# Gated memory two heads at a time, output products rounded, norms behind the products

## The chip, the cores and the metric

One NeuronCore of a Trainium2 chip runs the whole program. The time is that of the device, in microseconds (us), and for each kernel the median of its runs is given. Before the change: 3743.09 us, the median of 3 runs (3741.81 to 3745.54).

## What is computed

A sequence of 512 tokens of width 1024 passes through two blocks of two layers each. All of it is float32.

```
first block, per layer:   h += 0.5 g1 * swiglu(norm(h)...)      # FFN, width 2816
                          h += g2 * mixer(norm(h)...)           # fox + DSA heads (hyb), then MLA
                          h += 0.5 g3 * swiglu(norm(h)...)
                          ... at the end h = norm(h) * final_g
second block, per layer:  u = norm(h) * norm1_g ;  y = u @ w_in
                          h += concat(gated memory, diff attention, gated recurrence) @ w_out
                          h += relu(norm(h) * norm2_g @ w_up)**2 @ w_down
gated memory, per head:   D[t,s] = b_t - b_s + i_s   (s <= t)
                          S = (q k' / 8) * exp(D - m_t)
                          out = (S v) / max(|sum_s S|, exp(-m_t)),  then a norm and a gate
```

A norm divides each token's row by the root of the mean of its squares. It is a factor per token, so it can be applied to `u` before a product or to `y` behind it.

## The kernel before

**Layout.** The residual `h` is held as 8 chunks of 128 features by 512 tokens, and so is `u`, the input of a layer; `big` holds 32 such chunks. A layer is a list of weight slabs (`ORDER`): SP loads them into a ring of four slots, each load waiting until the slab four places back is done (`lin_done`). PE makes a group of products per slab into one of two PSUM pairs (`LP[0]`, `LP[1]`), DVE takes the group out (`lin_taken0`, `lin_taken1`) and PE may use the pair again.

**Rounded products.** In most layers (`CUT`) each f32 operand is split in a rounded high part and the remainder, and a product is made as three passes: high by high, high by low, low by high (`products`, L474). ACT rounds the weights (`high`, L1062, a copy into `w_hi`, two homes in turn, which waits until the slab two places back *in the list of rounded slabs* is done), and POOL subtracts (`rest`, L1419) in place over the ring (`w_lo`, `w_cut`). The output layers `hybo`, `mlao`, `wo0`, `wo1` (four slabs each, 64 products of 128x512) are not split: PE multiplies in f32 straight from the ring.

**A norm.** When a chunk of `h` is final, ACT squares it (`hrms`, L1107), POOL adds the squares (`squares`, L1468), PE sums over partitions (`total_sum`, L542), ACT takes the root, DVE the reciprocal (`root_total`), PE spreads it over the partitions (`spread`, L555), DVE scales the 8 chunks (`scale_in`, L1625), ACT rounds each, and only then PE starts the next layer's first slab with high passes and, at its end, the low ones (L502). The parameter `cut_at` says ahead of which chunk's square the first two slabs of the next layer are rounded; ACT and POOL keep the same order. In front of the second block two such norms follow each other: the final one of the first block and norm1 of layer 0.

**Attentions.** `duo_attention` (fox and DSA heads) takes two heads in a step: scores in both row halves of the array, and value products in both column halves. `attention` (MLA, diff) takes one. Each step goes PE, DVE, ACT, DVE, PE, ACT, PE.

**Gated memory** (L999 to L1013 for PE, L1376 for ACT, L2251 for DVE). 16 steps, one for each head and block of 128 keys. PE spreads the head's gate row once a head; per step DVE adds the causal mask to one block, ACT makes `E = exp(gate + bias)` (two instructions), PE the scores (64 rows), DVE `S = scores * E / 8`, PE the numerators (64 output rows) and the denominators (4 output rows). Between the steps stand the norms of the other two mixers: six sums (n = 5), a root and a reciprocal, and six spreads and scalings, one a step (n = 8 to 13). Then `out_products` makes the output layer: chunks 2 to 7 of slabs 0 and 1, between them the sum and the spread of the numerators' norm, then chunks 0 and 1, then slabs 2 and 3.

**Order.** Every engine has its program written out by hand; the semaphores named above are the only order between them. Each queue is in order.

Of the kernel before, what the change touches and what calls it, by code (L numbers as in the profile page):

```python
# [27 lines left out]
P = 128  # L28
# [135 lines left out]
class Fresh:  # L164


    def __init__(self, high, first):
        self.high, self.first = high, first
# [17 lines left out]
def build(nc, x, small, consts, consts2, pos, adab, w, out):  # L186
    with ExitStack() as ctx:
# [109 lines left out]

        def root4(b=0, n=1):
            return st[:, 58 + b:58 + b + n]
# [40 lines left out]
        def ffn_order(up, down, ada, more=0):  # L340
# [4 lines left out]
        ORDER += [("hyb", 10, DC * 256, 0, 1), ("hybv", 4, DC * 256, 0, 1), ("hybo", 4, DC * 256, 0, 0)]  # L345
        ORDER += ffn_order("gu01", "dn01", FC // 2) + ffn_order("gu10", "dn10", FC // 2)
        ORDER += [("mlad", 3, DC * 256, 0, 1), ("mlaq", 6, 3 * 256, 0, 0), ("mlak", 4, 2 * 256, 0, 0),
                  ("mlav", 4, 2 * 256, 0, 0), ("mlao", 4, DC * 256, 0, 0)]
        ORDER += ffn_order("gu11", "dn11", 0)
        for l in range(DEPTH):  # L350
            ORDER += [(f"in{l}", 11, DC * 256, 0, 1), (f"inv{l}", 4, DC * 256, 0, 1), (f"wo{l}", 4, DC * 256, 0, 0)]
            for part in "ab":
                ORDER += [(f"up{l}{part}", 8, DC * 256, 0, 1), (f"down{l}{part}", DC, 16 * P, 0, 1)]
# [3 lines left out]
        CUT_SLABS, slabs = [], 0  # L357
        for name, n, width, _, two in ORDER:
            CUT_SLABS += [(slabs + k, width) for k in range(n if two else 0)]
            slabs += n  # L360

# [5 lines left out]
        def peeled(pl, name, n, n_ada):  # L367

            if name in SLAB_ORDER:
                return n  # L370
            return 4 if pl.slab == 0 else n_ada if 0 < n_ada < n else None
# [83 lines left out]
        def _(pe):  # L455
# [11 lines left out]
            def linear(name, kind, src, after=None, fresh=None, amid=None):  # L467
# [13 lines left out]
                def body(k, it):  # L481
# [4 lines left out]
                    if cut:  # L486
                        pe.wait_ge(s("w_cut"), at(pl.cut + k + 1, it, RING))
                        high, rest = w_hi[:, (pl.cut + k) % 2, 0:width], w_lo[:, slot, 0:width]
# [13 lines left out]
                    elif kind == "fm" and k == 0 and fresh is not None:  # L502
# [39 lines left out]
            def total_sum():  # L542
# [3 lines left out]
                pl.got("squares_summed")  # L546
                for b in range(NB):
                    mm(XB[1][:, b:b + 1], sqa[:, blk(b)], cc("ones", 0, 1), start=b == 0, stop=False)
                pl.got("h_squared", DC)
                for b in range(NB):  # L550
                    last = mm(XB[1][:, b:b + 1], sq[:, (DC - 1) % 2, blk(b)], cc("ones", 0, 1), start=False, stop=b == NB - 1)
# [3 lines left out]
            def spread():  # L555

                pe.wait_ge(s("rstd_ready"), pl.norm)
                for b in range(NB):
                    last = mm(XB[0][:, blk(b)], root4(b).to_broadcast([P, P]), cc("ident"))
                last.then_inc(s("rstd_spread"), 1)  # L560

            def norm(high, summed=False):
# [5 lines left out]
                pl.ur += DC  # L568

                def src(c):  # L570
                    return high[:, c, :], u_lo[:, c, :]
                return src, fresh
# [200 lines left out]
            linear("hybo", "fm", lambda c: u[:, c, :])  # L773
# [60 lines left out]
            linear("mlao", "fm", lambda c: u[:, c, :])  # L834
# [4 lines left out]
            total_sum()  # L839
            spread()  # L840
            for l in range(DEPTH):
                src, fresh = norm(u_hi2)
# [127 lines left out]
                u0 = l * 4 * NB  # L970

                def weighted(n):

                    hh, b = divmod(n, NB)
                    pe.wait_ge(s("ms_ready"), u0 + n + 1)
                    mm(XB[hh // 2][half(hh), b * P:T], xv[:, b, 64 * hh:64 * hh + 64], S[:, n % 2, 0:T - b * P],
                       start=b == 0, stop=b == NB - 1)
                    mm(XB[2][0:4, b * P:T], full_sums(hh, 4), S[:, n % 2, 0:T - b * P],
                       start=n == 0, stop=n == 4 * NB - 1).then_inc(s("m_out"), 1)

                def mix_norms(n):

                    if n == 5:
                        pl.got("mix_squared", 3)
                        for c in range(DIFF_H):
                            mm(XB[3][0:8, :], full_sums(c, 8), Z[:, c, :], start=c == 0, stop=False)
                        for cp in range(2):
                            last = mm(XB[3][0:8, :], half_sums(2 + cp, 8), tabs[:, 2 + cp, :], start=False, stop=cp == 1)
                        last.then_inc(s("mix_summed"), 1)
                    if 8 <= n < 14:  # L990
                        i = n - 8
                        if i == 0:
                            pl.got("mix_recip")
                        else:
                            pe.wait_ge(s("mix_scaled"), 6 * l + i)
                        weights = cc("ident")[0:8, i:i + 1].to_broadcast([8, P]) if i < DIFF_H else halves_of(i - 2)
                        mm(XB[3][:, :], weights, mix_rows).then_inc(s("mix_spread"), 1)

                for n in range(4 * NB + 1):  # L999
                    hh, b = divmod(n, NB)  # L1000
                    if n < 4 * NB:
                        if b == 0:
                            if l * 4 + hh:
                                pe.wait_ge(s("g_taken"), l * 4 + hh)
                            mm(LP[1][:, 0, :], cc("ident")[0:4, hh:hh + 1].to_broadcast([4, P]),
# [1472 lines left out]
```

## Time and profile before

| | |
|---|---|
| median of 3 runs | 3743.09 us |
| profiled execution | 3749.99 us |
| its span | 3748.2 us |
| mean granted clock of TensorE | 0.963 |
| PE busy | 3597.0 us (96%) |
| DVE, ACT, POOL busy | 37%, 26%, 40% |

The profile is of one execution, and its own time stands 6.9 us above the median. A granted clock of 1.00 is 2.4 GHz, 0.50 is 1.2 GHz. An f32 product leaves two matmul records, a rounded pass one. The length of a matmul record includes its way through the array, so spacings are read from the starts.

### The profile page before, as it was taken

Reading aid. Unit: us, or ns where it says so; the run is one execution under the profiler, and the core shown is the slowest. Engines: PE = TensorE matmul, PEld = TensorE weight load, DVE = VectorE, ACT = ScalarE, POOL = GpSimd, SP = SyncE. Lnnn points to the kernel's source line nnn. Section 1 sums busy time; section 2 is a strip of 40 time slices with the busy share of each in tenths; the row PEclk is TensorE's granted clock in tenths of the full one; section 3 lists DMA queues with packets and bytes.
Section 4 is the critical chain, followed back from the end, with each engine's and each line's share of the span. In section 5 each row is a group of like instructions: output and inputs, shape, how many; then the busy total and the mean of one; then the engine's idle time right before and its main releaser. Section 6 shows DMA issues by size and latency. Waiting matters only on the chain.

```text
span 3748.2 us, 41071 instructions
## 1 busy us (share of the span) xinstructions
PE 3597.0 (96%) x16200; PEld 2740.0 (73%) x16200; DVE 1385.3 (37%) x2572; ACT 965.4 (26%) x1205; POOL 1490.6 (40%) x521
## 2 busy tenths in 40 slices
PE   8999999799999999999999989989999999799999
PEld 7878777558887888755688866843888869437887
DVE  4454277624243422233210145752201267632010
ACT  2222222522223212303222233331212233312221
POOL 3445451025454545400354554401546445014453
PEclk9999998899999999999999989988999999799999
DMA  6434221025343433220223222101222212002222
GB/s 247 184 140 177 98 79 57 1 79 191 119 190 114 189 123 136 81 99 12 79 80 105 88 76 79 68 1 45 90 91 100 90 68 79 12 34 79 101 90 79
DMA packets 53863, 360.58 MB, mean 96 GB/s; under 512 B 5968, under 2 KB 6352, under 8 KB 16592
## 3 DMA queue, kind: packets, MB, share of 16 engines
q1 hardware_dynamic: 53712, 358.53, 26.4%
q8 instruction: 100, 1.64, 0.2%
q14 instruction: 51, 0.42, 0.0%
HBM read 356.41 MB, written 2.10 MB: 96 GB/s over the span
## 4 chain that ended last, share of the span: by engine, by line
PE 90%; DVE 6%; ACT 1%; issue 1%; DMA 1%; POOL 1%; SPq 0%; DVEq 0%; ACTq 0%; POOLq 0%
PE LP L459 80%; PE XB L459 9%; DVE S L1814 1%; PE LP L747 1%; DMA big<-w_ada 1%; PE XB L631 0%; ACT E L1060 0%; DVE tmp L1936 0%; DVE st L1934 0%; POOL wk L1481 0%; ACT sq L1060 0%; DVE wk L1834 0%; DVE gain L1651 0%; DVE stat L1826 0%; POOL w_lo L1423 0%
## 5 line engine op out<-in xcount | busy, mean ns | idle before, releaser
L1423 POOL TENSOR_TENSOR w_lo<-ring,w_hi 128x2048 fp32r<-128x2048 f32 (+1 forms) x263 | 1122.9, 4270 | 682.8 <-ACT w_hi L1060 682.0
L459 PE MATMUL LP<-u_hi,w_hi 128*128 128x512 f32 x2480 | 992.9, 400 | 21.2 <-ACT u_hi L1060 17.0
L459 PE MATMUL LP<-u_hi,w_lo 128*128 128x512 f32 x2480 | 980.5, 395 | 0.0
L459 PE MATMUL LP<-u_lo,w_hi 128*128 128x512 f32 x2480 | 937.6, 390 | 0.0
L459 PE MATMUL LP<-big_r,w_hi 128*128 128x512 f32 x2432 | 749.6, 389 | 1.2 <-POOL w_lo L1423 1.2
L1060 ACT ACTIVATE w_hi<-ring 128x2048 fp32r<-128x2048 f32 (+1 forms) x263 | 468.7, 1782 | 813.9 <-PE LP L459 726.1
L459 PEld LDWEIGHTS LP<-u_hi,w_hi 128*128 128x128 f32 x2480 | 475.5, 192 | 137.3 <-issue 39.1
L459 PEld LDWEIGHTS LP<-u_hi,w_lo 128*128 128x128 f32 x2480 | 474.9, 192 | 102.2
L459 PEld LDWEIGHTS LP<-u_lo,w_hi 128*128 128x128 f32 x2480 | 467.0, 188 | 95.2 <-issue 0.5
L459 PEld LDWEIGHTS LP<-big_r,w_hi 128*128 128x128 f32 x2432 | 455.9, 188 | 95.6 <-issue 1.3
L459 PE MATMUL LP<-big_r,w_lo 128*128 128x512 f32 x1216 | 473.2, 389 | 0.0
L1464 POOL TENSOR_TENSOR big_r<-tmp,big_r 128x512 f32 (+2 forms) x120 | 192.5, 1604 | 687.6 <-DVE big_r L1667 687.6
L1481 POOL TENSOR_TENSOR wk<-wk,sq 128x512 f32<-128x512 f32 x66 | 84.7, 1284 | 697.2 <-ACT sq L1060 694.2
L1060 ACT ACTIVATE tmp<-LP 128x512 f32<-128x512 f32 (+1 forms) x121 | 86.1, 711 | 971.1 <-PE LP L459 971.1
L1672 DVE TENSOR_TENSOR tmp<-tmp,LP 128x512 f32<-128x512 f32 x88 | 60.6, 688 | 635.1 <-ACT tmp L1060 620.7
L459 PEld LDWEIGHTS LP<-big_r,w_lo 128*128 128x128 f32 x1216 | 228.3, 188 | 47.7
L459 PE MATMUL LP<-u,ring 128*128 128x512 f32 x512 | 224.7, 600 | 4.2 <-DVE u L2284 2.6
L1580 DVE SCALAR_TENSOR_TENSOR XB<-ada_in,csil,XB 128x256 f32<-128x256 f32 x390 | 191.1, 490 | 13.7
L459 PEld LDWEIGHTS LP<-u,ring 128*128 128x128 f32 x512 | 97.7, 192 | 128.8 <-issue 122.6
L1742 DVE SCALAR_TENSOR_TENSOR h<-LP,gate,h 128x512 f32 (+1 forms) x64 | 48.1, 751 | 357.0 <-PE LP L459 356.5
L1060 ACT ACTIVATE E<-S,stat 128x128 f32<-128x128 f32 (+3 forms) x160 | 89.2, 558 | 241.4 <-DVE stat L1817 161.8
L2296 DVE TENSOR_TENSOR tmp<-tmp,LP 128x1024 f32<-128x1024 f32 x32 | 39.1, 1222 | 280.9 <-ACT tmp L1060 280.9
(266 smaller groups left out, 3259.8 us busy)
## 6 DMA issues: line engine op xcount, KB each, us to landing
ada_in<-w_ada SPq DMA_DIRECT2D x66, 1024.0 KB, 4.9
ring<-w_in SPq DMA_DIRECT2D x22, 1024.0 KB, 4.8
ring<-w_gu00a SPq DMA_DIRECT2D x11, 1024.0 KB, 7.1
ring<-w_gu00b SPq DMA_DIRECT2D x11, 1024.0 KB, 6.6
ring<-w_gu01a SPq DMA_DIRECT2D x11, 1024.0 KB, 6.8
ring<-w_gu01b SPq DMA_DIRECT2D x11, 1024.0 KB, 6.7
ring<-w_gu10a SPq DMA_DIRECT2D x11, 1024.0 KB, 6.7
ring<-w_gu10b SPq DMA_DIRECT2D x11, 1024.0 KB, 7.0
```

Of the source, the lines that this page charges most:

```text
L459: return pe.matmul(o, lhsT=lhsT, rhs=rhs, start=start, stop=stop)
L747: last = pe.transpose(LP[1][:, j, blk(b)], E[:, 2 * (k % 2) + j, blk(b)], cc("ident"))
L1060: return act.activation(o, i, fn, **kw)
L1423: gp.tensor_tensor(w_lo[:, slab % RING, 0:width], ring[:, slab % RING, 0:width], w_hi[:, q % 2, 0:width].bitcast(F32), ALU.subtract).then_ ...
L1464: gp.tensor_tensor(big_r[:, lo, :], src, big_r[:, hi, :].bitcast(F32), ALU.subtract)\
L1481: gp.tensor_tensor(sqa, sqa, sq[:, c % 2, :], ALU.add).then_inc(s("sq_added"), 1)
L1580: ins = stt(part if c < DC - 1 else ada_acc[:, :], wv[:, c * 256:(c + 1) * 256], csil[:, c:c + 1], part, ALU.mult, ALU.add)
L1672: tt(o, tmp[:, p, 0:T].unsqueeze(1), LP[p][:, 1:2, :], ALU.mult))
L1742: stt(o, LP[p][:, 0:1, :], g, o, ALU.mult, ALU.add).then_inc(s(f"lin_taken{p}"), 1)
L1814: link(dve.tensor_tensor_reduce(out=S[:, k % 2, 0:W], in0=XB[k % 2][:, 0:W], in1=mask(qb, W), scale=1.0, scalar=LOWEST, op0=ALU.add, op1=A ...
L2296: cut_hidden(k, it, p, pl.low, 2, lambda o: tt(o, o, LP[p][:, :, :], ALU.mult))
```

## The change

- The four output layers are in `CUT`. Their inputs (`u`, after the attention) are rounded chunk by chunk by ACT (`high_mixed`) and the remainder made by POOL (`rest_mixed`), in the steps of the attention or the memory that come before; the chunk with the numerators is last. The rounded weights of these layers have two homes of their own in `big` (`HIGH_CHUNKS`).
- The norms in front of `in0`, `up0`, `in1`, `up1` are late (`late_rms`, `late_input`): ACT rounds `h * gain` unscaled, PE makes the high passes of slab 0, then the sums, then the low passes, then the spread; DVE copies the spread row to `R` and multiplies by it whatever comes out of the products. In front of `in0` both norms are made from one pass over `h` (`twice`): squares of `h` and of `h * final_g`, during the last down layer.
- In `up`, DVE makes `max(y, 0) * R` and ACT the square; before, ACT made the relu and DVE the square. The `up` layers' loops are written out.
- The gated memory has 8 steps of two heads. All four gate rows are spread first; one instruction makes `E` per head; six spreads and scalings stand at n = 5 to 8, the sums at n = 3.

The diff, cut to its core:

```diff
-        ORDER += [... ("hybo", 4, DC * 256, 0, 0)]            # likewise mlao, wo{l}
+        ORDER += [... ("hybo", 4, DC * 256, 0, 1)]
+        HIGH_CHUNKS = {"hybo": (FK, FV), "mlao": (0, KN), "wo0": (AQ, AK), "wo1": (AQ, AK)}
...
@@ PE, first slab of a layer behind a norm
+                        if fresh.late:
+                            total_sum(fresh.late)
                         for c in range(n_c):
                             pe.wait_ge(s("u_ready"), fresh.first + c + 1)
...
                     last.then_inc(s("lin_done"), 1)
+                    if k == 0 and fresh is not None and fresh.late:
+                        spread(fresh.late)
...
@@ PE, gated memory
                 def weighted(n):
+                    cp, b = divmod(n, NB)
                     pe.wait_ge(s("ms_ready"), u0 + n + 1)
+                    W, sn = T - b * P, (S, ET)[n % 2]
+                    for j in range(2):
+                        hh = 2 * cp + j
+                        mm(XB[cp][half(j), b * P:T], xv[:, b, 64 * hh:64 * hh + 64], sn[:, j, 0:W],
+                           start=b == 0, stop=b == NB - 1)
+                    for j in range(2):
+                        last = mm(XB[2][0:4, b * P:T], full_sums(2 * cp + j, 4), sn[:, j, 0:W],
+                                  start=n == 0 and j == 0, stop=n == 2 * NB - 1 and j == 1)
...
+                for hh in range(4):
+                    mm(XB[hh][:, :], cc("ident")[0:4, hh:hh + 1].to_broadcast([4, P]), gate_row(1))
+                for n in range(2 * NB + 1):
+                    cp, b = divmod(n, NB)
+                    if n >= 5:
+                        mix_spread(2 * n - 10 if n < 8 else 5)
+                    if n < 2 * NB:
+                        if n >= 2:
+                            pe.wait_ge(s("ms_ready"), u0 + n - 1)
+                        for j in range(2):
+                            last = mm(LP[n % 2][:, j, 0:T - b * P], big[half(j), XK + cp, blk(b)],
+                                      big[half(j), XQ + cp, b * P:T])
+                    if n:
+                        weighted(n - 1)
+                    if n == 3:
+                        mix_sums()
+                    if 5 <= n < 7:
+                        mix_spread(2 * n - 9)
...
-                out_products(1, range(2, DC))
+                out_products(1, range(2, 6))
                 pl.got("num_recip")
...
+                out_products(1, range(6, DC))
...
@@ ACT
+            def late_chunk(c, gains, twice):
+                f(u_hi2[:, c, :], h[:, c, :], ACT.Copy, scale=gains[:, c:c + 1]).then_inc(s("u_high"), 1)
+                ...
+                f(square_home(c, True), h[:, c, :], ACT.Square).then_inc(s("h_squared"), 1)
+                if twice:
+                    ...
+                    f(square_home(c, True, True), h[:, c, :], ACT.Square, scale=sp_("final_g", c)).then_inc(s("seconds"), 1)
...
+            def behind_dsa(n):
+                if n == 1:
+                    cut_output("hybo", 3)
+                if n in (3, 5):
+                    high(pl.cut + (n - 3) // 2)
+                if n in (7, 11, 15):
+                    cut_output("hybo", n // 4 + 3)
...
+            def beside_heads(n):
+                if n % NB == 3 and NB < n < 8 * NB:
+                    cut_output("mlao", n // NB - 1)
+                if n in (9, 21):
+                    high(pl.cut + n // 21)
...
+                    for j in range(2):
+                        hh = 2 * cp + j
+                        f(E[:, 2 * (n % 2) + j, 0:T - b * P], wk[:, hh, b * P:T], ACT.Exp,
+                          bias=tokw[:, 4 * b + hh:4 * b + hh + 1]).then_inc(s("me_done"), 1)
...
+                    if n in (1, 2):
+                        high(pl.cut + n - 1)
...
@@ POOL, in front of up{l}: the order of the queue
+            def late_squares(cut_at=(7,), twice=False):
+                for c in range(DC - 2 if twice else 1, DC):
+                    if c == DC - 1:
+                        gp.nop().then_inc(s("squares_summed"), 1)
+                        ...
+                    for j, chunk in enumerate(cut_at):
+                        if chunk == c:
+                            rest(pl.cut + j)
+                    if c == DC - 1:
+                        break
+                    late_square(c, twice)
...
@@ DVE
+                for c in range(DC):
+                    pl.got("u_high")
+                    stt(u_lo[:, c, :], h[:, c, :], gains[:, c:c + 1], u_hi2[:, c, :].bitcast(F32), ALU.mult, ALU.subtract)
...
+                pl.got("rstd_spread")
+                link(dve.tensor_copy(R, XB[0][:, :]))
...
+                    else:
+                        tt(big[:, c:c + 2, :], LP[p][:, :, :], over_two(R), ALU.mult).then_inc(s(f"lin_taken{p}"), 1)
                     if k == 0:
                         gates_begin()
+                        for i in range(DC) if l == 0 else ():
+                            stt(h[:, i, :], h[:, i, :], sp_("final_g", i), XB[3][:, :], ALU.mult, ALU.mult)
...
+                    link(tt(qk_rows(i), XB[0][0:8, :], R[0:8, :], ALU.mult))
+                    tt(qk_rows(i), qk_rows(i), R[0:8, :], ALU.mult).then_inc(s("qk_means"), 1)
```

## Rows read from the trace of the kernel before

**Rows 1.** The page: busy time, share and instructions of PE; the chain by engine.
```profile
PE 3597.0 (96%) x16200; PEld 2740.0 (73%) x16200; DVE 1385.3 (37%) x2572; ACT 965.4 (26%) x1205; POOL 1490.6 (40%) x521
...
PE 90%; DVE 6%; ACT 1%; issue 1%; DMA 1%; POOL 1%; SPq 0%; DVEq 0%; ACTq 0%; POOLq 0%
```
**Rows 2.** Stretches: us, PE busy (records), granted clock, DMA share, GB/s.
```profile
2488.60:2547.60 59.00, 57.67 (x129) 0.83 0.00 0
...
2611.10:2636.00 24.90, 19.19 (x75) 0.73 0.12 43
3379.80:3403.40 23.60, 17.89 (x73) 0.78 0.12 45
2972.90:2993.90 21.00, 18.06 (x74) 0.76 0.14 51
2185.40:2222.00 36.60, 22.56 (x97) 0.67 0.08 29
```
**Rows 3.** PE in order of time, hybo: start, length, ..., [idle before].
```profile
746.56 55.20 PE L459 MATMUL LP<-u,ring 128*128 128x512 f32 x128 [0.79 <-DVE u L1853]
805.50 1.84 PE L459 MATMUL XB<-cst,wk 128*128 128x1 f32 x8 [3.74 <-POOLq L1474]
```
**Rows 4.** PE in order of time, wo0, and wo1's last 40 products.
```profile
2547.59 10.57 PE L459 MATMUL LP<-u,ring 128*128 128x512 f32 x24
...
2573.68 37.42 PE L459 MATMUL LP<-u,ring 128*128 128x512 f32 x80 [1.31 <-DVE u L2284]
2614.66 1.83 PE L459 MATMUL XB<-cst,wk 128*128 128x1 f32 x8 [3.55 <-POOLq L1474]
...
3345.19 34.60 PE L459 MATMUL LP<-u,ring 128*128 128x512 f32 x80 [1.31 <-DVE u L2284]
```
**Rows 5.** PE in order of time, first slab of in0.
```profile
2208.78 0.63 PE L459 MATMUL LP<-u_hi,w_lo 128*128 128x512 f32 x1
2209.20 0.63 PE L459 MATMUL LP<-u_hi,w_hi 128*128 128x512 f32 x1
...
2218.38 3.79 PE L459 MATMUL LP<-u_lo,w_hi 128*128 128x512 f32 x16
2222.01 0.39 PE L459 MATMUL LP<-u_hi,w_hi 128*128 128x512 f32 x1
```
**Rows 6.** ACT and POOL in order of time, first slab of up0.
```profile
2585.99 1.89 ACT L1060 ACTIVATE w_hi<-ring 128x2048 fp32r<-128x2048 f32 x1
...
2588.42 4.50 POOL L1423 TENSOR_TENSOR w_lo<-ring,w_hi 128x2048 fp32r<-128x2048 f32 x1
```
**Rows 7.** DVE in order of time, the numerators' norm of wo0.
```profile
2560.07 0.68 DVE L2278 SCALAR_TENSOR_TENSOR ada_in<-XB,ada_in 4x512 f32<-4x512 f32 x1 [10.28 <-PE XB L459]
...
2561.97 3.34 DVE L2282 RECIPROCAL ada_in<-ada_in 4x512 f32<-4x512 f32 x1
```
**Rows 8.** Groups by line and form: busy us, mean ns | idle before.
```profile
L1060 ACT ACTIVATE sq<-h 128x512 f32<-128x512 f32 x77 | 46.2, 622 | 117.3 <-DVE h L1767 46.5 <-POOL wk L1481 29.4 <-DVE h L2287 26.0
...
L1481 POOL TENSOR_TENSOR wk<-wk,sq 128x512 f32<-128x512 f32 x66 | 84.7, 1284 | 697.2 <-ACT sq L1060 694.2
...
L2296 DVE TENSOR_TENSOR tmp<-tmp,LP 128x1024 f32<-128x1024 f32 x32 | 39.1, 1222 | 280.9 <-ACT tmp L1060 280.9
...
L2162 DVE TENSOR_SCALAR big<-LP 128x1024 f32<-128x1024 f32 x14 | 17.1, 1225 | 41.0 <-PE LP L459 41.0
```
**Rows 9.** PE in order of time: a pair in the DSA heads; the gated memory.
```profile
713.36 1.13 PE L459 MATMUL XB<-big 64*128 64x512 f32 x4
...
2501.58 1.12 PE L459 MATMUL LP<-big 64*128 64x512 f32 x2
...
2527.08 0.86 PE L459 MATMUL XB<-S,big 128*64 128x384 f32 x2
2527.87 0.81 PE L459 MATMUL XB<-S,ada_in 128*4 128x384 f32 x2
```
**Rows 10.** Group by line and form: the attentions' exponentials of 512 columns.
```profile
L1060 ACT ACTIVATE E<-S,stat 128x512 f32<-128x512 f32 x40 | 28.7, 719 | 51.9 <-DVE stat L1817 36.0 <-DVE stat L1864 10.3 <-PE LP L747 5.3
```

More of the change, by code:

```diff
@@ L164, with __init__ @@
 class Fresh:
-    def __init__(self, high, first):
-        self.high, self.first = high, first
+    def __init__(self, high, first, late=0):
+        self.high, self.first, self.late = high, first, late
 def at(value, it, per):
@@ L560, in spread, with mixed, src, input_of @@
                 last.then_inc(s("rstd_spread"), 1)
+            def mixed(name):
+                ready = set()
+                def src(c):
+                    if c not in ready:
+                        ready.add(c)
+                        pl.got("mix_cut")
+                    return mixed_high(name, c), u_lo[:, c, :]
+                return src
+            def input_of(high):
+                def src(c):
+                    return high[:, c, :], u_lo[:, c, :]
+                return src
             def norm(high, summed=False):
@@ L772, in _ @@
             pe.wait_ge(s("o_taken"), pl.head)
-            linear("hybo", "fm", lambda c: u[:, c, :])
+            linear("hybo", "fm", mixed("hybo"))
             ffn("gu01", "dn01")
@@ L833, in _ @@
             pe.wait_ge(s("o_taken"), pl.head)
-            linear("mlao", "fm", lambda c: u[:, c, :])
+            linear("mlao", "fm", mixed("mlao"))
             ffn("gu11", "dn11")
             pe.wait_ge(s("const2_in"), 16)
-            total_sum()
-            spread()
             for l in range(DEPTH):
-                src, fresh = norm(u_hi2)
+                src, fresh = late_norm(twice=l == 0)
                 first = pl.group
@@ L981, in mix_norms @@
[L981 to L997, printed above, removed]
@@ L1159, in ffn @@
                         f(st[:, 46:50], st[:, 42:46], ACT.Exp).then_inc(s("lam_exp"), 1)
-                    layer(down + part, angles if up + part == "gu00a" else None, last=part == "b")
+                    layer(down + part, angles if up + part == "gu00a" else None, last=part == "b",
+                          behind=final_chunk if down + part == "dn11b" else None)
             def angles(k, it):
@@ L1288, in _ @@
             skip("mlav")
-            attention(MLA_H, 192.0 ** -0.5, P)
-            skip("mlao")
+            def beside_heads(n):
[3 more added lines that the diff above has]
+                    high(pl.cut + n // 21)
+            attention(MLA_H, 192.0 ** -0.5, P, beside=beside_heads)
+            cut_output("mlao", 7)
+            layer("mlao", last=True)
             ffn(1, 2, "gu11", "dn11", 2)
-            hrms()
-            pl.tu += DC
             for l in range(DEPTH):
-                if l:
-                    hrms()
-                else:
-                    hrms(cut_at=(), normed=True)
-                high(pl.cut + 1)
-                high_input(u_hi2)
+                late_rms(sp_("norm1", l * DC, DC) if l else gain, twice=l == 0)
                 first = pl.group
@@ L1494, in ffn, with final_square @@
                     layer(up + part, low_hidden(FC // 2, 1))
-                    layer(down + part, last=part == "b")
+                    layer(down + part, last=part == "b", behind=final_square if down + part == "dn11b" else None)
+            def final_square(k):
+                if 1 <= k < DC - 2:
+                    late_square(k, True)
             def turn(chunks, t, home=S):
@@ L1518, in _ @@
             layer("hybv", last=True)
-            skip("hybo")
+            rest_mixed("hybo", 0, 1, 2, 3)
+            rest(pl.cut)
+            rest(pl.cut + 1)
+            rest_mixed("hybo", 4, 5, 6, 7)
+            layer("hybo", last=True)
             ffn("gu01", "dn01", (4, 6))
```

380 lines of the change are left out of this document (256 added, 124 removed).

## The prediction

> **What bounds the kernel now.** I read the page's first part, then the chain that ended last, then stretches of PE, then the order of time around the places that the diff touches. PE is busy 96% of a 3748.2 us span and the chain of waits is PE for 90% [rows 1]. So time goes away only where PE has fewer passes to make, where it stands still, or where its granted clock is half. The reader should see three such kinds. The stretches around the norms and the gated memory have a clock of 0.67 to 0.83 [rows 2]. In front of each ordinary norm PE stands 3.55 or 3.74 us, put down to the POOL queue, and then sums and spreads at half clock [rows 3, 4]. And the output projections take 55.20 us for 128 records; one f32 product is two records, so 64 products of 0.863 us [rows 3].
>
> **Output products in three rounded passes** (hybo, mlao, wo0, wo1; 64 products each). Sixteen rounded passes start over 2222.01 - 2218.38 = 3.63 us, 0.227 us a pass; at half clock a pass takes 2209.20 - 2208.78 = 0.42 us [rows 5]. Three passes are 0.68 us, a slab of 48 is 10.9 us, a layer 43.7 us.
>
> hybo and mlao: 55.2 to 43.7 us, 11.5 us less each (mlao repeats the row of hybo). What is given back: the first slab of the next FFN may now be rounded only when the buffers of the last rounded products are free, and those are the output slabs. ACT's rounding of its second slab (1.89 us) and POOL's remainder (4.50, some 0.5 after it [rows 6]) therefore run after the last output product T, and both stand in their queues ahead of the squares of chunk 6 and of POOL's last addition (1.28 [rows 8]). The sum is then ready at T + 0.1 + 1.9 + 0.5 + 4.5 + 1.3 = T + 8.3, and not T + 3.74 as now [rows 3]. POOL may start nearer to ACT's end, so I take 4.3 us lost on each of these two ordinary norms. Beside the attentions ACT gets seven copies of 0.62 and two roundings of 1.89, 8.1 us, and POOL some 18 us. Hidden entirely they cost 0; if all of ACT's is in the ring DVE, ACT, PE it is 8.1. MLA leaves PE hardly idle and I take 1; the fox and DSA heads hand every step around the three engines, I take 3. The last chunk's copy and remainder (0.62 + 1.28) lie under the first 14 products, 9.6 us. Net: hybo 11.5 - 4.3 - 3 = 4.2, mlao 11.5 - 4.3 - 1 = 6.2.
>
> wo0 and wo1: now 2547.59 to 2614.66 - 3.55 = 2611.11, 63.5 us, and in the second layer 3319.10 to 3379.79, 60.7 (the first fell to a lower clock behind its stall of 1.31: 37.42 against 34.60 us for 80 records) [rows 4]. After: products of chunks 2 to 7 of slab 0, 12 x 0.683 = 8.2; the numerator's sum 1.8 (2558.2 to DVE's start after it [rows 4, 7]); 8 products of slab 1, 5.5, which cover DVE's 0.68 + 1.26 + 3.34 from 2560.07 to 2565.31 [rows 7]; the spread 2.0; 4 products 2.7 while DVE multiplies (1.22 [rows 8]), ACT copies two chunks (1.0) and DVE subtracts (1.2), 3.6 with the hops, so a stall of 0.9; 8 products 5.5. Now slab 2: its rounded weights go to the home that slab 0 used, so ACT starts when slab 0 is done, 1.9 + 0.5 + 4.5 = 6.9, of which the last 4 products of slab 1 cover 2.7: a new stall of 4.1 us. Slabs 2 and 3, 21.8. Sum 52.5 us: 11.0 and 8.2 less. Half clock behind the new stall (the row at 37.42 shows 2.8 lost behind 1.31 of standing) can cost 0 to 3.4; I take 1.5 each. Net 16.2.
>
> **Norms behind products** (the four norms of the second block). Chunks are rounded unscaled as soon as each is final, products start at once, and the row R multiplies what comes out.
> - Before in1: now 20.9 us from the last down product to the end of slab 0 [rows 2]. After: 32 high passes 7.3, the sum's 8 small products 1.9, 16 low passes 3.6, spread 1.2: 14.0. The root is ready under the low passes. 6.9 less.
> - Before up0 and up1: 24.8 and 23.6 now [rows 2]. The same 14.0, but squares_summed stands behind the same rounding and remainder at T + 8.3, so PE waits 1.0 after its 7.3: 15.0. R comes 0.6 late for slab 2's remainder (POOL has 0.5 us of slack there now), 0.6 more. 9.2 and 8.0 less.
> - Before in0, where two norms follow each other: 36.6 us now, at a clock of 0.67 [rows 2]. After: POOL's remainder of slab 0 ends about 1.8 us after the last down product (chunk 6's copy and two squares, 0.63 each, then 1.9, then 4.5, from 2178 on, one slab of 7.5 us before the end), high passes 7.3, two sums 3.8, low passes 3.6, two spreads 2.3: 18.9. The second root, with DVE's three small steps, fits in the 3.6. 17.7 less. In each of the six down slabs before, POOL has 3.2 + 2 x 1.28 = 5.8 of 7.48 us.
> What this adds in the in layers: scaling by R replaces a tensor_scalar of 1.23 by a tensor_tensor of 1.22 [rows 8]; two more 8-row products per root, about 2 us twice, and 8 operations on h, 5.4 us once, all on DVE in slabs 0 to 4 where it has more than half of each slab idle. Cost 0, as PE's slab needs its bank only two slabs on; if the cover failed, 2 x 2 + 5.4 = 9.4. In up, squaring moves from DVE to ACT behind DVE's max: DVE, ACT, DVE, as long as ACT, DVE, DVE: 0. Unrolled up loops: 0, from -1 to 1, no row shows a loop's end costing PE anything. in0 to up1 together 17.7 + 6.9 + 17.2 = 41.8.
>
> **Gated memory, two heads at a time.** Now 59.0 us, at a clock of 0.83 [rows 2]; the second layer is the same. On halves: a pair of 64-row scores of 512 columns, 4 records, takes 1.13 in the fox/DSA attention, and a single one in today's loop 1.12 [rows 9]: the pair costs one. A change of form costs something: a group of 384 columns and the next start 0.79 apart where the columns alone, four times at 2.4 GHz, are 0.64 [rows 9]. The Trainium skill, TensorEngine Tiling (Array Packing), Key Properties, says that changing the tiling mode (not the tile alone) drains TensorE, which speaks against a loop that changes it three times a step; the trace agrees, with 0.15 us here. By the rule taken at its worst, a drain of 0.2 at each of 24 changes, the loop would be 1.2 us longer than by my spacings.
> PE's work at full clock after: scores 1.06, 0.92, 0.70, 0.49; numerators in column halves, bounded by one single (side by side) and two (serial), taken as one: 1.06, 0.79, 0.58, 0.36; denominators serial 1.8, 1.4, 0.96, 0.53; together 10.6 for four steps, 21.3 for eight. Gate rows 3.6, norm sums 5.2, six spreads 6.3: 36.4. Then the waits. DVE copies two pairs of gate rows (2 x 1.22), adds the mask (0.42); ACT makes two exponentials (0.72 each [rows 10]); DVE 0.42 + 1.24: the first numerators start at 8.6 with 2.9 of standing. Behind the norm sums, root and reciprocal (0.7 + 3.3 [rows 7]) hold spread 0 for 2.3. From there on spreads, DVE's scalings and DVE's S alternate, 7.5 more. 36.4 + 12.7 = 49.1 at full clock. Now about a third of the loop runs at half clock (2 x (1 - 0.83)); after, some of that falls in the waits; I take 4: 53.1. 5.9 less, twice, 11.8. Bounds: all clock hidden, 49.1 (9.9 less); all PE work of a third at half clock, 49.1 + 12 = 61.1 (2.1 more).
>
> **Sum.** 4.2 + 6.2 + 16.2 + 41.8 + 11.8 = 80.2 us, made against the profiled execution's 3749.99 us (span 3748.2 and 1.8 around it): 3669.8. That execution is 6.9 above the median 3743.09, so the median becomes **3663 us**.
>
> **Rivals.**
> 1. The memory loop gains nothing: two heads make each hand-over longer (two exponentials before one S), and six scalings fall in four steps, not six. For it: 12.7 us of waits in my own sum. Against it: fewer passes where PE is busy 57.67 of 59.00 now [rows 2]. 3663 + 11.8 = 3675.
> 2. The cuts are not hidden: ACT's 8.1 us is in the ring of both attentions (4 counted, 16.2 paid: + 12.2) and half clock follows each new stall at 3.4 instead of 1.5 (+ 3.8): 3679; with rival 1 it is 3691. For it: every step there passes ACT twice, with the exponentials and with the copy of what was transposed. The Trainium skill, GPSIMD Engine Reference, Specifications, says that GpSimd shares its SBUF interfaces with VectorE and contends with its two-input operations; no row shows POOL beside this attention, and the rule points towards this rival's time.
> 3. Better: memory at 49.1 twice (- 8), attentions free (- 4), no clock lost (- 3): 3648.
> 4. The other side: half clock in the new passes. The stalls before slab 2 and at the mixed chunks bring the clock down in the output layers, and 768 passes run at 0.42 and not 0.227, 0.193 x 768 = 148 us: 3811. It decides from 80.2 / 0.193 = 416 of the 768 on. Against it: behind a wait of over 10 us the passes are at 0.42 at 2208.8 and at 0.227 from 2218.4 on at the latest [rows 5].
> 5. It does not do what it says: halves run one after the other (+ 11.8), products still stand in front of the norms (+ 41.8), the cuts are not hidden (+ 16.0) and DVE's additions are not either (+ 9.4): 3742, no change.
>
> **Chances.** Forecast 0.58 (its own range 3645 to 3680), rival 1 0.15, rival 2 alone or with 1 0.12, better 0.08, slower 0.05, nothing 0.02. 0.2%, 7.5 us, is what a measurement of this kernel tells from no change. Faster 0.93, same 0.02, slower 0.05. Range 3630 to 3705: from rival 3 with 18 us for what is mis-sized below, to rivals 1 and 2 together with 14 above.
>
> **What would show it.** hybo and mlao 44 us from first to last product; the sum of gu01 and gu11 8 us behind it; in wo a stall near 4 us before slab 2; slab 0 of in1 ended 14 us after the last down product, of in0 19, of up0 and up1 15 to 16; the memory loop 53 us with pairs of scores near 1.1; clock in those norm stretches above 0.9. I am wrong if the output passes are apart by more than 0.25 us, if POOL's remainder ends much later than named, if DVE in the in layers holds a bank that PE wants, or if the attentions before hybo and mlao grow by more than 8 us.

## The result, and the profile after

The changed kernel takes 3709.19 us (median of 4, 3708.42 to 3710.31), the kernel before 3744.32 us beside it: ratio 0.9902, 95% interval 0.9888 to 0.9916. So it is 35 us faster where 80 were forecast, and 3709 lies above the range's upper end of 3705. The profiled execution took 3708.42 us with a span of 3706.6, against 3749.99 and 3748.2; the account below is made between these two. They are 41.6 us apart, 6.4 more than the medians: the one before stands 5.7 above its median here, the changed one 0.8 below.

The page of the changed kernel, busy time by engine and the chain by engine; it answers to [rows 1]:
```profile
PE 3537.7 (95%) x16456; PEld 2785.3 (75%) x16456; DVE 1423.0 (38%) x2526; ACT 1006.5 (27%) x1222; POOL 1603.5 (43%) x565
...
PE 88%; DVE 6%; issue 2%; ACT 2%; POOL 1%; DMA 1%; SPq 0%; DVEq 0%; ACTq 0%; POOLq 0%
```
PE lost 59 us of busy time, the span only 41.6: PE stands still 18 us more than before.

**What came as forecast.** The changed kernel's PE in stretches (us, PE busy (records), granted clock, DMA share, GB/s): hybo, then in0 from its first product to the end of the spread; the latter answers to the last row of [rows 2]:
```profile
747.17:791.00 43.83, 43.83 (x192) 1.00 0.31 120
...
2188.84:2205.13 16.29, 16.29 (x97) 1.00 0.12 45
```
hybo is 43.8 us from first to last product for 55.2 [rows 3], with the clock at 1.00. The sum of the next norm then stands 8.35 us, where 3.74 stood [rows 3]; the forecast said 8.3. In in0 the last down product ended at 2186.13 and slab 0 and spread at 2205.13: 19.0 us for 36.6 [rows 2], as forecast, though PE stood 2.71 us ahead of it where the forecast had 1.8. In in1 slab 0 and spread took 13.5 us (2944.68 to 2958.17), where 14 were forecast. PE in order of time, changed kernel:
```profile
799.35 0.99 PE L483 MATMUL XB<-cst,wk 128*128 128x1 f32 x4 [8.35 <-POOLq L1660]
...
2188.84 0.47 PE L483 MATMUL LP<-u_hi,w_hi 128*128 128x512 f32 x1 [2.71 <-POOL w_lo L1572]
```

**What did not: the MLA attention.** It took 91.26 us where it took 79.65. Stretches: the whole attention of the kernel before, then of the changed kernel the whole and the 10 us behind one stall:
```profile
1678.53:1758.18 79.65, 75.27 (x368) 1.00 0.08 31
```
```profile
1673.10:1764.36 91.26, 81.04 (x369) 0.93 0.07 27
1701.00:1711.00 10.00, 9.24 (x33) 0.66 0.00 0
```
Of the 11.6 us, 5.8 are idle PE (10.2 for 4.4) and 5.8 are longer busy time at a clock of 0.93. The first of its two stalls, in VectorE's, GpSimd's and TensorE's order of time:
```profile
1690.80 0.49 DVE L2056 TENSOR_SCALAR E<-E,stat 128x512 f32<-128x512 f32 x1
...
1696.31 4.66 DVE L2056 TENSOR_SCALAR E<-E,stat 128x256 f32<-128x256 f32 x1
...
1696.32 4.50 POOL L1572 TENSOR_TENSOR w_lo<-ring,big_r 128x2048 fp32r<-128x2048 f32 x1 [3.62 <-ACT big_r L1130]
...
1701.11 0.41 PE L686 MATMUL XB<-cst,E 128*128 128x128 f32 x2 [2.64 <-DVE E L2056]
```
The reader should see one instruction of VectorE, half as wide as the one of 0.49 us above it, that takes 4.66 us and ends 0.15 us behind GpSimd's. In the other six of its form at this line it is 0.35. Such a long instruction is called a hold below. The second, at 1731.37, repeats it to the hundredth.

**The memory loop.** It was to fall from 58.9 to 53.1 us and took 61.05 and 61.35. First the kernel before (its second loop is the same), then the changed one; both answer to the first row of [rows 2]:
```profile
2488.65:2547.59 58.94, 57.66 (x129) 0.83 0.00 0
```
```profile
2472.23:2533.28 61.05, 49.33 (x129) 0.72 0.00 0
3225.85:3287.20 61.35, 49.14 (x129) 0.72 0.00 0
```
Pairing took its passes away: busy time times mean clock, an estimate of the work at full clock, falls from 47.9 to 35.5 us (I had 36.4). But PE now stands 11.7 us for 1.3, and the lower clock costs by the same estimate 13.8 us (49.33 - 35.5) for 9.8. PE's waits in the first loop, from the first spread on:
```profile
2501.32 1.49 PE L483 MATMUL XB<-ada_in,cst 8*128 8x512 f32 x2 [2.19 <-DVE ada_in L2507]
2504.79 1.97 PE L483 MATMUL XB<-S,big 128*64 128x512 f32 x4 [0.39 <-DVE S L2503]
2511.48 1.40 PE L483 MATMUL XB<-ada_in,cst 8*128 8x512 f32 x2 [0.84 <-DVE u L2476]
...
2524.88 1.12 PE L483 MATMUL XB<-S,big 128*64 128x256 f32 x4 [2.53 <-DVE S L2503]
2531.71 0.69 PE L483 MATMUL XB<-ET,big 128*64 128x128 f32 x4 [1.90 <-DVE ET L2503]
```

**wo0, wo1 and the norms behind them.** wo0 took 56.63 us, wo1 56.9, where the forecast had 54.0 with the clock term; slab 0 of up0 ended 17.0 us behind the last product where it had 15.0. Stretches (wo0; slab 0 of up0; of that the part behind its wait), then the two waits:
```profile
2533.28:2589.91 56.63, 52.58 (x201) 0.92 0.15 56
2589.91:2606.91 17.00, 15.33 (x73) 0.90 0.18 63
...
2599.00:2606.91 7.91, 7.91 (x40) 0.78 0.00 1
```
```profile
2566.44 0.47 PE L483 MATMUL LP<-big_r 128*128 128x512 f32 x1 [4.05 <-POOL w_lo L1572]
...
2599.00 1.02 PE L483 MATMUL XB<-cst,rstd 128*128 128x1 f32 x8 [1.67 <-POOLq L1641]
```
The stall of 4.05 ahead of slab 2 is the one forecast. The wait for the squares' sum is 1.67 us where I had 1.0, and what follows it has a clock of 0.78: the 16 low passes took 5.49 us, where 3.6 were forecast.

### The profile page after: what moved, and what is told of

Read it like the earlier page. It is cut to its first block, busy times and chain, and to the rows that moved or that the text cites. A ratio compares the mean times of both kernels' runs of the same rounds, so it can differ in the third digit from the quotient of the medians.

```text
span 3706.6 us, 41386 instructions
## 1 busy us (share of the span) xinstructions
PE 3537.7 (95%) x16456; PEld 2785.3 (75%) x16456; DVE 1423.0 (38%) x2526; ACT 1006.5 (27%) x1222; POOL 1603.5 (43%) x565
## 4 chain that ended last, share of the span: by engine, by line
PE 88%; DVE 6%; issue 2%; ACT 2%; POOL 1%; DMA 1%; SPq 0%; DVEq 0%; ACTq 0%; POOLq 0%
PE LP L483 78%; PE XB L483 9%; POOL w_lo L1572 1%; DVE S L2042 1%; PE XB L686 1%; PE LP L802 1%; DMA big<-w_ada 1%; ACT E L1130 1%; DVE tmp L2164 0%; DVE st L2162 0%; ACT w_hi L1130 0%; DVE gain L1878 0%; ACT big_r L1130 0%; ACT sq L1130 0%; DVE wk L2062 0%
## 5 line engine op out<-in xcount | busy, mean ns | idle before, releaser
L483 PE MATMUL LP<-big_r,w_lo 128*128 128x512 f32 x1472 | 576.4, 392 | 0.0
L483 PEld LDWEIGHTS LP<-big_r,w_lo 128*128 128x128 f32 x1472 | 278.5, 189 | 58.5
L1130 ACT ACTIVATE tmp<-LP 128x512 f32<-128x512 f32 x89 | 53.3, 599 | 705.3 <-PE LP L483 705.3
L1572 POOL TENSOR_TENSOR w_lo<-ring,big_r 128x2048 fp32r<-128x2048 f32 x16 | 73.0, 4571 | 257.2 <-ACT big_r L1130 257.2
L1579 POOL TENSOR_TENSOR u_lo<-u,big_r 128x512 fp32r<-128x512 f32 x28 | 36.2, 1300 | 274.8 <-ACT big_r L1130 274.8
L2546 DVE TENSOR_TENSOR h<-h,LP 128x512 f32 x32 | 22.0, 687 | 317.0 <-PE LP L483 317.0
L483 PE MATMUL XB<-big 64*128 64x128 f32 (+5 forms) x472 | 128.3, 511 | 15.1 <-DVE stat L2045 5.0
```

The lines of the kernel that those rows point to most:

```text
L483: return pe.matmul(o, lhsT=lhsT, rhs=rhs, start=start, stop=stop)
L1130: return act.activation(o, i, fn, **kw)
L1572: gp.tensor_tensor(w_lo[:, slab % RING, 0:width], ring[:, slab % RING, 0:width], w_high(q, width).bitcast(F32), ALU.subtract).then_inc(s(" ...
L1579: gp.tensor_tensor(u_lo[:, c, :], u[:, c, :], mixed_high(name, c).bitcast(F32), ALU.subtract)\
L2546: tt(o, o, LP[p][:, 0:1, :], ALU.add).then_inc(s(f"lin_taken{p}"), 1)
```

## The experiments

Each ratio is to the kernel before, measured beside the run; that kernel's median was 3744.32 us beside the changed kernel and 3745.10 to 3749.18 beside the experiments, so they compare by ratio better than by time. Stretches are of one execution each, and some differ where the kernel is the same. In the traces that leave these stages as in the changed kernel, the first memory loop took 61.0 to 63.4 us, the second 59.5 to 66.0, and the MLA attention 90.5 to 91.7. The code cuts are shortened.

**MLA.** Theory A: VectorE stands as long as the GpSimd instruction beside it runs. Theory B: it is ScalarE's roundings in the ring of the attention, the mechanism of my rival 2.

```
-            rest_mixed("mlao", 0)
-            rest(pl.cut)
-            rest_mixed("mlao", 1, 2, 3)
-            rest(pl.cut + 1)
-            rest_mixed("mlao", 4, 5, 6, 7)
+            rest_mixed("mlao", 0, 1, 2, 3, 4, 5, 6, 7)
+            rest(pl.cut)
+            rest(pl.cut + 1)
```


> The changed kernel with one thing moved: GpSimd's two subtractions that make the lower parts of mlao's first two weight slabs (4.50 us each) stand behind the MLA attention, after the eight subtractions for its outputs, where they stood beside it. ScalarE's two weight roundings and its output roundings stay in the attention. The changed kernel's time is 3709.2 us, its MLA attention 91.3 us (79.7 before). Theory A (a VectorE instruction that reads and writes SBUF stands still as long as a GpSimd instruction runs beside it, and TensorE's clock falls in the stall): the attention falls to 80 to 83 us; the output pass starts some 4.5 to 6 us later after it; time 3702 to 3706. Theory B (ScalarE's roundings of 1.9 us in the ring are what lengthens the attention): it stays at 90 to 92 us, and the later start comes on top: 3713 to 3716.

3710.0 us, ratio 0.9898 (0.9883 to 0.9913), outside the ranges of theory A (3702 to 3706) and theory B (3713 to 3716). The attention's PE from first to last, and what the output pass then waits for:
```profile
1673.58:1752.44 78.86, 75.26 (x368) 1.00 0.08 30
```
```profile
1759.88 0.77 PE L483 MATMUL LP<-big_r 128*128 128x512 f32 x1 [7.44 <-POOL w_lo L1572]
```
With all of ScalarE's roundings still in it, the attention is back at the length and clock of before: theory B falls. Of the 12.4 us of gain the later start takes 9.3: 7.44 us of waiting for 0.78, and an output pass and wait for the sum of 54.6 us for 51.9 behind it. I had 4.5 to 6. The first memory loop, which the edit doesn't touch, was 2.4 us longer in this execution (63.4), and with both the time missed its range.

```
+                for i in range(2):
+                    gp.tensor_tensor(sq[:, :, :], <half i of the slab>, <half i of its upper part>, ALU.subtract)
                 gp.tensor_tensor(w_lo[...], ring[...], w_high(q, width), ALU.subtract)
```


> The changed kernel with GpSimd's work beside the MLA attention doubled: ahead of each of the two weight subtractions stand two more of 128x1024, of the same operands, into a buffer that nobody reads. Nothing is added on another engine. Theory A (VectorE's scaling of the probabilities stands while a GpSimd instruction runs): each added instruction of about 2.3 us can hold one scaling, and the clock falls again: the attention goes from 91.3 to 97 to 103 us, time 3715 to 3721. Theory B (ScalarE's roundings): the attention stays at 91 to 92 us, time 3709.

3715.3 us, ratio 0.9917 (0.9903 to 0.9930). The median is in theory A's range, but not for its reason: the attention stayed at 90.5 us, where 97 to 103 were forecast. The profiled execution, the shortest of five (3709.26 to 3720.97), has a span of 3707.5, 0.9 more than the changed kernel's; what the others lost is open. VectorE and PE:
```profile
1696.98 2.50 DVE L2068 TENSOR_SCALAR E<-E,stat 128x256 f32<-128x256 f32 x1
1702.49 4.16 DVE L2068 TENSOR_SCALAR E<-E,stat 128x512 f32<-128x512 f32 x1
...
1702.14 0.52 PE L686 MATMUL XB<-cst,E 128*128 128x128 f32 x3 [1.23 <-ACT ET L1130]
...
1706.79 0.63 PE L686 MATMUL XB<-cst,E 128*128 128x128 f32 x4 [2.63 <-DVE E L2068]
```
The holds are there, two large ones for one. The first stands beside a GpSimd instruction of 2.34 us, the second starts 0.64 us into the one of 4.51 us and ends 0.29 us behind it. Behind the hold of 2.50 PE waits only 1.23, put down to ScalarE. In all PE stands 12.3 us for 10.2, and its busy time is 2.8 us shorter at a clock of 0.96 for 0.93. So what a hold costs isn't the sum of GpSimd's work: the long instruction costs 2.63 again, the added ones 1.23. Why the clock was higher is open.

```
+                for i in range(4):      # wo, hybo, mlao: 128x2048 as four of 128x512
+                    a, b = i * width // 4, (i + 1) * width // 4
+                    ins = gp.tensor_tensor(w_lo[:, slot, a:b], ring[:, slot, a:b], w_high(q, width)[:, a:b], ALU.subtract)
```


> The changed kernel with GpSimd's weight subtractions beside the three attentions and memory loops (hybo, mlao, wo0, wo1: two slabs each, 128x2048, 4.50 us) cut into four instructions of 128x512 each; same bytes, same order. Theory A with a hold per instruction: VectorE's waits shrink from 4 us to about 1 us: the MLA attention 91.3 to 82 to 85 us, each memory loop 61 to 55 to 58 us, time 3692 to 3700. If VectorE gets no turn between GpSimd's instructions: no change, 3709. Theory B (ScalarE's roundings, and the hand-overs of the paired loop): no change in either place, 3708 to 3712.

3702.17 us, ratio 0.9875 (0.9860 to 0.9890). VectorE, GpSimd, and stretches of PE: the MLA attention, then the first memory loop:
```profile
1702.13 1.43 DVE L2066 TENSOR_SCALAR E<-E,stat 128x256 f32<-128x256 f32 x1
...
1702.15 5.12 POOL L1581 TENSOR_TENSOR w_lo<-ring,big_r 128x512 fp32r<-128x512 f32 x4 [3.62 <-ACT big_r L1130]
```
```profile
1678.94:1758.85 79.91, 74.79 (x368) 1.00 0.07 30
2467.64:2530.00 62.36, 50.44 (x128) 0.69 0.00 0
```
In pieces the hold is 1.43 us, about one piece long; PE's longest wait beside the pieces is 0.74 us for 2.64, and the attention's 11.4 us are back with GpSimd's work unmoved: theory A holds, per instruction. The time is 2.2 us above its range (3692 to 3700), since the memory loop, which was to fall to 55 to 58 us, doesn't gain; its loss has another cause. The fox and DSA attention became 1.9 us longer (128.8 for 126.9, and 126.6 to 127.6 in the other traces); in the trace five of VectorE's scalings there are held for 1.1 to 1.5 us, where the changed kernel has three of 1.1 to 2.6. Whether that is the cause is open.

**The memory loop.** Theory 1: the cuts beside it take its gain. Theory 2: its own waits do.

```
-                for n in range(2 * NB + 1):      # two heads a step
+                for n in range(4 * NB + 1):      # the loop of before; ScalarE rounds weights at n = 2 and 4
```


> The changed kernel with the memory loop of the kernel before: one head at a time, 16 steps, scores of one row half alone; the rounded output products, the weight cuts of ScalarE and GpSimd beside the loop, and the late norms stay. Theory 1 (pairing is worth the predicted 5.9 us a layer, and GpSimd's subtractions take it away again in the loop, whichever loop it is): the loop becomes longer than the changed kernel's 61 us, 65 to 68 us, time 3717 to 3723. Theory 2 (pairing by itself brings nothing or costs: hand-overs twice as long in half as many steps): the loop takes 59 to 62 us, time 3705 to 3711.

3713.92 us, ratio 0.9914 (0.9901 to 0.9928), between the ranges of the two (3705 to 3711 and 3717 to 3723). PE in the first and second loop:
```profile
2472.30:2540.50 68.20, 66.77 (x128) 0.70 0.00 0
3231.50:3293.10 61.60, 59.45 (x129) 0.81 0.00 0
```
The single loop with the cuts beside it is 2.7 to 9.3 us longer than without them (58.9), nearly all of it clock. Against the paired loops of the changed kernel that is 0.3 and 7.2 us more, but the paired ones differ by as much between traces, so what pairing alone is worth this run doesn't settle.

```
-        (f"wo{l}", 4, DC * 256, 0, 1)       # rounded in three passes
+        (f"wo{l}", 4, DC * 256, 0, 0)       # whole fp32; no cuts on ScalarE, GpSimd, VectorE
```


> The changed kernel with the output products wo0 and wo1 in whole fp32 as before: no weight cuts and no output cuts for them on ScalarE, GpSimd and VectorE; the memory loop stays paired (two heads a step). So the paired loop runs with nothing of the rounding beside it. Theory 1 (pairing is worth what was predicted, and the cuts beside it take it away): the loop falls from 61.1 and 61.3 us to 53 to 55; the products take 63.5 and some 61 us again for 56.6 and 56.9, time 3704 to 3708. Theory 2 (the paired loop has its own waits: the six spreads and scalings of the output norms, two to a step now, and the product S behind them on VectorE, and a lower clock in them): the loop stays at 58 to 61 us, time 3716 to 3720.

3718.94 us, ratio 0.9923 (0.9907 to 0.9940). The paired loops with nothing of the rounding beside them:
```profile
2474.60:2535.90 61.30, 50.44 (x129) 0.69 0.00 0
3230.90:3294.10 63.20, 52.78 (x128) 0.66 0.00 0
```
No shorter than with the cuts (61.05 and 61.35): theory 1 falls. That the paired loop's own waits do it, theory 2, is tested by the next run. This one also gives the rounding of wo alone: 0.9923 against 0.9902, about 8 us where the forecast had 16.2 for it; the two intervals overlap.

```
# TensorE                                      # VectorE
-  mix_spread(...)                             -  mix_scale(...)
   scores(n)                                      S(n - 1)
+  mix_spread(...)                             +  mix_scale(...)
   weighted(n - 1)                                mix_scale(...)
```


> The changed kernel with two orders changed in the paired memory loop, nothing added or left out: TensorE spreads the root of the output norms behind the step's scores instead of ahead of them, and VectorE makes the step's gated product (S) ahead of its output scalings instead of behind the first. Theory 2 (ping-pong of spread and scaling, and the product behind them): of the loop's 11.7 us of waits, the 8.5 behind the first spread go, and the clock with them: the loop falls from 61.1 to 51 to 55 us, time 3693 to 3700. Theory 1 (the cuts of ScalarE and GpSimd beside the loop): the loop stays at 59 to 61 us, time 3706 to 3710.

3690.08 us, ratio 0.9847 (0.9831 to 0.9864), 3 us below theory 2's range. Both loops, and what is left of the waits in the first from the first spread on:
```profile
2474.64:2526.70 52.06, 47.56 (x128) 0.75 0.00 0
3218.10:3267.30 49.20, 45.09 (x129) 0.79 0.00 0
```
```profile
2503.70 1.43 PE L483 MATMUL XB<-ada_in,cst 8*128 8x512 f32 x2 [1.34 <-DVE ada_in L2505]
...
2512.81 1.12 PE L483 MATMUL XB<-ada_in,cst 8*128 8x512 f32 x2 [0.21 <-DVE u L2476]
...
2519.75 1.12 PE L483 MATMUL XB<-ada_in 8*128 8x512 f32 x2 [0.42 <-DVE u L2476]
```
Same instructions, other order: 9.0 and 12.2 us less. Of these 7.2 and 8.1 are waits (11.7 and 12.2 to 4.5 and 4.1), 1.8 and 4.1 the clock that came with them. The scaling now stands under the scores, and S no longer stands behind a scaling. So theory 2 stands for the waits. The low clock mostly stays: with work of 35.7 and 35.6 us by the same estimate it costs 11.9 and 9.5 us. The loops are now 1 and 4 us below the 53.1 forecast, but by luck: the forecast had 12.7 us of waits and 4 of clock.

**The norms.**

```
-                cut_at = (4, 6) if per == 2 else (7,)
+                cut_at = (4,) if per == 2 else (7,)      # likewise on GpSimd, and for up0, up1
```


> The changed kernel with the second weight slab of gu01, gu11, up0 and up1 cut behind the last square of the norm, on ScalarE and on GpSimd, where it was cut two chunks before it. Forecast: the waits for the sums, 8.35 and 8.06 us at gu01 and gu11, fall by GpSimd's 4.5 us each, those of 1.67 at up0 and up1 go; the second cut is hidden by the norm and the first slab. Time 3696 to 3701. Rival: ScalarE's squares, not GpSimd's additions, end the wait, or the second slab comes late: 3706 to 3710.

3702.61 us, ratio 0.9869 (0.9848 to 0.9890). The waits for the sums of gu01 and gu11:
```profile
797.68 1.43 PE L483 MATMUL XB<-cst,wk 128*128 128x1 f32 x8 [3.81 <-POOLq L1660]
...
1811.33 1.33 PE L483 MATMUL XB<-cst,wk 128*128 128x1 f32 x8 [3.80 <-POOLq L1660]
```
4.5 and 4.3 us less, and slab 0 of up0 and up1 ends 13.5 us behind the last output product for 17.0: in all 15.8 us, where 8 to 13 of time were forecast. The median is still 1.6 us above its range. In the profiled execution (3704.38) stages that the edit doesn't touch took more than in the changed kernel: the second memory loop 66.0 us, and in0 with inv0 4.9 more. Another execution took 3689.9; what differs between them is open.

```
-    HIGH_HOME: slabs 2 and 3 of wo over the upper parts of slabs 0 and 1
+    HIGH_HOME: slabs 2 and 3 of wo in w_hi, rounded behind the numerators' squares and their root
```


> The changed kernel with another home for the upper parts of the third and fourth weight slab of wo0 and wo1: they are rounded into the buffer that the memory loop has just left, not over those of the first two slabs, so ScalarE needn't wait for the first slab's last product (it rounds the third behind the squares of the numerators, the fourth behind their root). Theory (the stall of 4.05 us ahead of the third slab is the chain of last product, rounding 1.9 and subtraction 4.5, and TensorE's half clock follows it): stall and low clock go, wo0 and wo1 fall from 56.6 and 56.9 us to 50 to 52, time 3696 to 3700. Rival (GpSimd is late by itself, since the output cuts come first): the stall stays, 3707 to 3710.

3704.28 us, ratio 0.9889 (0.9872 to 0.9905). wo0 and wo1:
```profile
2535.50:2586.30 50.80, 50.80 (x201) 0.94 0.17 62
3286.40:3337.20 50.80, 50.80 (x201) 0.94 0.17 63
```
The stall is gone, and 1.8 us of clock with it: 56.6 and 56.9 to 50.8, as forecast. The time isn't: 3696 to 3700 was its range. Slab 0 of up0 and up1 gave 1.6 back each (18.6 for 17.0): its wait of 1.67 is still there, and the clock behind it is 0.64 in 9.57 us, where it was 0.78 in 7.91.

**Together.** `combined` is the MLA attention in pieces, the late second cut and the reordered loop; `combined_homes` has the other home for wo as well.

> The changed kernel with three things together: GpSimd's two weight subtractions beside the MLA attention in pieces of 128x512, the second weight slab of gu01, gu11, up0 and up1 cut behind the last square, and the reordered paired memory loop. If the three are independent and each is worth what theory A and theory 2 say (11.4, 10 and 14 us): 3672 to 3680. If the memory loop doesn't gain: 3686 to 3690.

3659.25 us, ratio 0.9762 (0.9746 to 0.9778), below the range expected (3672 to 3680). Its loops took 49.2 and 53.8 us. By the stretches the gains add up: 11.4, 9.0 + 12.2 and 15.8 are 48.4 us, and the span is 49.2 below the changed kernel's. The expectation had 10 for the late cut and 14 for the loops.

> The combined kernel (pieces of 128x512 in the MLA attention, late second cut, reordered memory loop; 0.9762 of the time before) with the third and fourth slab of wo0 and wo1 in the other home. If the stall of 4.05 us and the half clock behind it go in both layers: 10 to 12 us less, a ratio of 0.973 to 0.974 to the kernel before. If the stall is only moved: 0.976.

3643.63 us, ratio 0.9723 (0.9707 to 0.9739), a little better than the 0.973 to 0.974 expected, and 101 us below the kernel before. Its first loop, wo0, and slab 0 of up0:
```profile
2457.50:2506.70 49.20, 45.09 (x129) 0.79 0.00 0
...
2506.70:2556.10 49.40, 49.40 (x201) 0.97 0.18 64
2556.10:2569.70 13.60, 13.60 (x74) 1.00 0.22 79
```

## Why the prediction was wrong

By its own terms, gain forecast and measured between the two profiled executions. Each stage is measured from its start to the start of what follows: in0 and in1 from the last down product to the memory loop, wo and up with their down layers.

| term | forecast | measured |
|---|---|---|
| fox/DSA attention, hybo, sum | 4.2 | 3.3 |
| MLA attention, mlao, sum | 6.2 | -5.6 |
| in0 and in1 | 24.6 | 23.1 |
| memory, two layers | 11.8 | -4.6 |
| wo0, wo1, up0, up1 | 33.4 | 23.6 |
| sum | 80.2 | 39.9 |

The spans differ by 41.6 us: 2.8 were gained ahead of the first stage and 1.1 lost in the FFNs between. Of the 40.3 us missing from the sum, the memory has 16.4, MLA 11.8 and wo and up 9.8.

- **Right:** the rounded pass at 0.227 us, hybo's 43.8 us, the 8.3 us wait for the sum, in0's 19 us (its terms add to 18.8, not 18.9), in1's 14, the stall of 4.1 us in wo, pairs of scores for the price of one (1.13 us for four records). The 3 us for the fox and DSA heads (3.4 measured) came true in size, but no run says which engine's work costs them.
- **The step that failed first: "MLA leaves PE hardly idle and I take 1."** It cost 11.6. I asked what ScalarE's copies do to the ring, and took GpSimd's 18 us as free because nobody in the ring waits for GpSimd. The runs show the opposite: ScalarE's share costs nothing (78.86 us with all of it), and the two 128x2048 subtractions cost 11.4 through VectorE. Rival 2 had 12.2 for both attentions together, near the 11.0 by which they exceeded my 4, but its sum is made of ScalarE's copies; it named VectorE and GpSimd only in a sentence beside it.
- I wrote that no row shows GpSimd beside this attention. That is so, but the same trace shows holds elsewhere, one of them in in0; VectorE and GpSimd:
```profile
2224.42 4.97 DVE L2073 SCALAR_TENSOR_TENSOR big<-big 4x512 f32<-4x512 f32 x1
...
2224.26 4.59 POOL L1423 TENSOR_TENSOR w_lo<-ring,w_hi 128x2048 fp32r<-128x2048 f32 x1 [13.62 <-ACT w_hi L1060]
```
  Four partitions by 512 in 4.97 us, where the same instruction takes 0.68 in the changed kernel, with no GpSimd instruction beside it (2211.05), and one of that shape (from PSUM) 0.68 [rows 7]. The Trainium skill, SBUF — State Buffer, "SBUF: two separate sides", calls the port pair that VectorE and GpSimd share an exclusive lock, held for the whole instruction by whichever starts first of a GpSimd operation and a VectorE operation in a 2-port mode or with two SBUF inputs. On the whole instruction the trace agrees: 4.66, 2.50 and 1.43 us of hold beside instructions of 4.50, 2.34 and about 1.3. On who started first it doesn't decide: in the attention VectorE's records start 0.01 to 0.02 us before GpSimd's, and still it is VectorE that waits.
- **The second, and the one with the largest price: the memory loop's clock, "I take 4".** Work (35.5 for 36.4) and waits (11.7 for 12.7) were sized well; the low clock cost 13.8. My own upper bound was 61.1 us, and that is what came: rival 1, but 2.1 and 2.4 us a layer worse than its price of no gain. The order that I read and priced but did not question, 7.5 us of spreads, scalings and S in turn, could be ordered away, and 1.8 and 4.1 us of clock went with it. The other 9.5 to 11.9 us of clock are still there, so the cause of most of this term stays open.
- **The third: wo and up.** The low clock in wo cost 4.2 us a layer (52.58 busy at 0.92, an estimate) where I took 1.5. Only part of it is the stall's: with the stall gone some 3 us stay (50.80 busy at 0.94), and wo0's first 7.7 us, right behind the memory loop, have a clock of 0.82. Behind the wait of 1.67 us in up the sums and low products ran at 0.78, 17.0 us for 15.0. Without the stall wo went below my forecast (50.8 for 54.0), and without the wait slab 0 of up did (13.5 for 15.0).
- **Open:** why the paired loop has a clock of 0.75 to 0.79 even when PE stands only 4 us in it; why one single loop took 68.2 us and the other 61.6; the 1.9 us in the fox and DSA attention with pieces; what makes executions of one kernel differ by 14.5 us (3689.9 to 3704.38).

## What to carry to other kernels

Work laid on GpSimd beside a ring that never waits for it isn't free: look for VectorE instructions with their data in SBUF next to it, and price the longest single GpSimd instruction against the slack of the ring; cutting it in four gave back 11.4 us there for 0.6 us more of GpSimd's time a slab. When a loop's steps are merged, list what each in-order engine now holds ahead of the critical product; here two swaps were worth 21 us in the two loops, over four times the 4.6 that the merging had lost. Beside a stall, count what it takes of TensorE's clock: here 0.25 to 1 times its length (1.8 on 7.2 us and 4.1 on 8.1 in the loops, 1.8 on 4.05 in wo, 5.8 on 5.8 in the MLA attention). And compare a single stage only with its spread over several traces.

## What the hardware showed that I had not expected

- VectorE operations that read PSUM were not held: in the memory loop, S (LP and E, 128x512) took 0.68 us at 2489.69, within GpSimd's 9.18 us (two instructions from 2484.94 on), while the mask's addition of two SBUF operands (128x256, 0.42 by itself) took 4.07 and 3.88 on either side of it.
- In the MLA attention a short hold costs less than its length: behind 1.43 us PE waited at most 0.74, behind 2.50 it waited 1.23, behind 4.66 us 2.64, and then a clock of 0.66 for 10 us.
- Taking 6 us of holds out of the memory loop (pieces) changed nothing in its length (62.4 us); taking 7 to 8 us of PE's waits out of it took 9 to 12.
